# Differential attention blocks with the most keys: the second softmax is multiplied on ScalarE and added on GpSimd, and the build-time order is made anew

## The chip, the cores and the metric

The kernel runs on 1 core of one Trainium2 chip. The metric is device time in microseconds (us) of one execution; the value of a kernel is the median of its runs.

## The reference, cut to what matters

A decoder block over 2048 positions and 1024 features, all in float32: input projection, two kinds of attention side by side, output projection, and an MLP with squared ReLU. The change is in the attention alone, and there in the differential kind (4 heads), whose core is:

```python
s = jnp.einsum('bqhnd,bkhnd->bhnqk', q_i, k).astype(jnp.float32) * scale   # n = 0, 1: two score maps
s = s + bias[None, :, None]
s = jnp.where(mask, s, -jnp.inf)
p = jax.nn.softmax(s, axis=-1)
a = p[:, :, 0] - lam * p[:, :, 1]                                          # the "mix"
o = jnp.einsum('bhqk,bkhd->bqhd', a.astype(v.dtype), v)
o = rmsnorm(o, g_sub) * (1.0 - lam_init)
```

The other kind (forgetting attention, "FOX", 8 heads) has one softmax for each head and no mix.

## The kernel before, in words

**Stages.** Projection runs up to about 565 us, attention from there to about 1410 us, output projection to about 1640 us, and the MLP fills the rest. Nothing outside attention is touched.

**Blocks.** Attention is a list of 48 blocks (`attention_blocks`). There are 8 units u; even ones are FOX (a pair of heads, sides s = 0 and 1, a block for each), odd ones are differential (one head, a block for each J). A block is 512 queries, J = 0 to 3; block J needs 4 J + 4 key tiles of 128, so J = 3 is the longest. A FOX unit takes J in the order 0, 1, 2, 3, a differential unit 1, 3, 2, 0. There are four differential heads, so four differential blocks with J = 3: the "long differential blocks" that the change names. In a differential block each of the four query tiles a = 3, 2, 1, 0 (in this order) has `keys` = (4 J + a + 1) * 128 keys: 2048, 1920, 1792 and 1664 at J = 3.

**Steps of a block.** TensorE forms the scores of a tile in parts of at most 1024 columns ("score"); VectorE takes the negated row maximum from PSUM ("max", L1333); ScalarE writes exp into SBUF and sums it ("exp", L1294). The first softmax goes to `probs`, a ring of 141 * 128 columns; the second goes to `probs1`, which has two buffers. Where a tile has two parts, the low part's maximum is old: ScalarE makes a factor ("corr", L1274), and GpSimd multiplies the low 1024 columns of the first softmax by it ("fix", L1207). When both softmaxes of a differential tile are there, VectorE makes two factors out of sums and lambda ("chain", five instructions of one column, L1354 to L1362), and then the tile is mixed: probs += probs1 * factor ("mix"). For tiles a = 1, 2, 3 GpSimd mixes: multiply the high columns (L1216), multiply the low 1024 (L1219), add the high (L1222), add the low (L1226); L1229 and L1232 where a tile has one part. For tile a = 0 (`DVE_TILES`) VectorE mixes with one fused instruction for each part, high at L1371, low at L1376. Then, for each key tile, TensorE transposes the four query tiles into PSUM ("turn", L1458), ScalarE copies them to SBUF as the high half of a split product ("hi", L1303), VectorE subtracts for the low half ("lo", L1342), and TensorE multiplies by v ("pv", L1473 to L1478). Transposes, low halves and a few small steps share a ring of 3 PSUM banks; scores have 2 buffers; `p_hi` and `p_lo` have 4.

**What sets the order.** Each engine runs its own instruction stream in order, and a wait at the head of a stream holds all that stands behind it. The order in which the steps of different blocks are interleaved in these streams is made when the kernel is built, by a planner (`Walk`, L797 to L850): each step has an engine, a time for which it holds the engine, a time after which its result is there, predecessors, and an urgency. The planner walks through a model of time and lets each free engine take the able step with the lowest urgency. A step's urgency is its block's number, moved on with its place in the block, plus a constant of its kind (`RUSH`, L857); scores of long differential blocks are moved forward by `EARLY` blocks (L946). SP's stream (loads of q, k, v and stores) comes from the same walk. Steps of one kind keep their own order. The order alone comes out of the walk; correctness rests on semaphore waits that each engine makes for itself.

Of the kernel before, what the change touches and what calls it, by code (L numbers as in the profile page):

```python
# [8 lines left out]
ALU = mybir.AluOpType  # L9
# [727 lines left out]
DVE_TILES = (0,)  # L737

# [42 lines left out]
def probability_columns(blocks):  # L781

    places, former, owner, at = {}, {}, [None] * (PROB_COLUMNS // P), 0
    for b in blocks:
        for a in (3, 2, 1, 0):
            n = 4 * b.J + a + 1
            if (at + n) * P > PROB_COLUMNS:
                at = 0
            former[b.n, a] = max((o for o in owner[at:at + n] if o is not None), default=None)
            owner[at:at + n] = [b.n] * n  # L790
            places[b.n, a] = at * P
            at += n
    return places, former


class Walk:
# [18 lines left out]
    def order(self):  # L815
# [62 lines left out]
def attention_steps(blocks, scores, turns):  # L878
# [30 lines left out]
    def variance(b, urgency):  # L909

        before = diffs.index(b) - 1
        walk.step("var", b, "PE", 0.25, urgency, [("o_sq", b), ring[-TRING]], 0.45, line="ring")
        walk.step("o_var", b, "DVE", 0.2, urgency,
                  [("var", b), ("rows", b), ("o_pow", diffs[before]) if before >= 0 else None], line="ring")
        ring.append(("o_var", b))
        walk.step("o_pow", b, "POOL", 1.1, urgency,
                  [("o_var", b), ("spread", b.qb - 2) if b.qb >= 2 else None])

    def finish(q, urgency):

        pair = pairs[q]
        walk.step("spread", q, "PE", 0.5, urgency,
                  [("rows" if b.kind == FOX else "o_pow", b) for b in pair] + [ring[-TRING]],
                  0.7, line="ring")
        walk.step("o_scale", q, "DVE", 0.7, urgency, [("spread", q)] + [("o_add", b) for b in pair], line="ring")
# [16 lines left out]
    for b in blocks:  # L942
        ahead, mine, fox = by_block[b.n], turns_of[b.n], b.kind == FOX
        load("load_q", q_blocks[b.qb], b.n - 2, [("score", last_q[b.qb - 2])] if b.qb >= 2 else ())
        for k, sc in enumerate(ahead):
            at = b.n - 1 + SPREAD * k / len(ahead) - LEAD - (EARLY if not fox and b.J == 3 else 0)  # L946
            parts, two, keys = parts_of[b.n, sc.a, sc.s], sc.parts == 2, sc.lo + sc.width
            for p in pieces_of(sc):
                load_piece("load_k", b.u, p, b.n - 2)
            walk.step("score", sc, "PE", 0.00089 * sc.width + 0.03, at + RUSH["score"],  # L950
                      [("exp", scores[sc.g - 2]) if sc.g >= 2 else None, ("load_q", q_blocks[b.qb])]
                      + [("load_k", (b.u, p)) for p in pieces_of(sc)], 0.00089 * sc.width + 0.25)
            walk.step("max", sc, "DVE", 0.16 + 0.00104 * sc.width + (0.2 if sc.part else 0), at + RUSH["max"],
                      [("score", sc)])
            if sc.part:
                walk.step("corr", sc, "ACT", 0.29, at + RUSH["corr"], [("max", sc)])
# [9 lines left out]
            walk.step("exp", sc, "ACT", 0.49 + 0.00083 * sc.width, at + RUSH["exp"], after)  # L966
            if sc.part and (fox or sc.s == 0):
                walk.step("fix", (b.n, sc.a), "POOL", 2.0, at + RUSH["fix"], [("corr", sc), ("exp", parts[0])])
# [10 lines left out]
        for k, t in enumerate(mine):  # L979
# [3 lines left out]
            else:  # L983
# [4 lines left out]
            walk.step("turn", t, "PE", 0.0012 * width, at + RUSH["turn"], after, 0.0012 * width + 0.17, line="ring")  # L988
            walk.step("hi", t, "ACT", 0.2 + 0.00083 * width, at + RUSH["hi"],
                      [("turn", t), ("pv", turns[t.n - PRING]) if t.n >= PRING else None])  # L990
            walk.step("lo", t, "DVE", 0.16 + 0.00104 * width, at + RUSH["lo"], [("hi", t)], line="ring")
# [3 lines left out]
                      cost + 0.2)  # L995
# [6 lines left out]
        if fox:  # L1002
            walk.step("o_half", b, "ACT", 0.6, end, [("pv", mine[-1])])
        else:
            d = diffs.index(b)
            walk.step("o_sq", b, "ACT", 0.6, end, [("pv", mine[-1]), ("var", diffs[d - 1]) if d else None])
        walk.step("o_add", b, "DVE", 0.69, end, [("o_half" if fox else "o_sq", b),
                                                ("store", b.qb - ORING) if b.qb >= ORING else None])
# [17 lines left out]
def attend(nc, ctx, keep, qk, vals, q_rows, k_rows, mixT, w_out, x):  # L1026
# [22 lines left out]
    tile_no, chain_done, mix_done = {}, {}, {}  # L1049
    chains, mixes = 0, {True: 0, False: 0}  # L1050
    for sc in scores:
        if blocks[sc.b].kind == DIFF and sc.s == 1 and sc.part == sc.parts - 1:
            tile_no[sc.b, sc.a] = len(tile_no)
            chains += 5 if sc.parts == 2 else 2
            on_dve = sc.a in DVE_TILES
            mixes[on_dve] += (2 if sc.parts == 2 else 1) * (1 if on_dve else 2)
# [16 lines left out]
    with ExitStack() as own:  # L1073
# [34 lines left out]
        mixed = sems.sem("mixed")  # L1108
        mixed_dve = sems.sem("mixed_dve")
# [22 lines left out]
        def wait_mixed(eng, b, a):  # L1132
            eng.wait_ge(mixed_dve if a in DVE_TILES else mixed, mix_done[b, a])
# [58 lines left out]
        def gpsimd(pool):  # L1192
# [7 lines left out]
            for what, arg in steps:  # L1200
# [8 lines left out]
                elif what == "mix" and arg[1] not in DVE_TILES:  # L1209
# [58 lines left out]
        def scalar(act, then):  # L1268
            first_hi = next(arg for what, arg in steps if what == "hi")
            for what, arg in steps:  # L1270
# [5 lines left out]
                elif what == "exp":  # L1276
# [43 lines left out]
        def vector(dve, then, between):  # L1320
# [8 lines left out]
            for what, arg in steps:  # L1329
# [35 lines left out]
                elif what == "mix" and arg[1] in DVE_TILES:  # L1365
# [934 lines left out]
```

## Time and profile before

| | |
|---|---|
| Median of 3 runs | 3008.07 us |
| Lowest and highest of them | 3007.61 and 3008.24 us |
| The profiled execution's own time | 3007.83 us |
| Its span, first to last instruction | 3005.8 us |
| Granted TensorE clock, mean | 0.992 of full speed |
| TensorE busy | 2914.9 us (97%) |
| VectorE busy | 1660.9 us (55%) |
| ScalarE busy | 1022.1 us (34%) |
| GpSimd busy | 977.5 us (33%) |

How to read it: PE is TensorE's matmuls, PEld its weight loads, DVE VectorE, ACT ScalarE, POOL GpSimd. The shares are averages over stages that differ: the MLP alone fills nearly half of the span. So what bounds the attention stage has to be read from stretches of that stage.

### The profile page before, as it was taken

To read this page: it belongs to the slowest core of one execution; us is meant where nothing else is said; L and a number is where in the kernel's file an instruction comes from. 1 tells how busy PE (TensorE), PEld (TensorE's weight loads), DVE (VectorE), ACT (ScalarE), POOL (GpSimd) and SP (SyncE) were. 2 spreads that over 40 slices of the span, in tenths; PEclk is the share of its full clock that TensorE was granted. 3 is DMA by queue.
4 is the path that set the end of the run, shared out by engine and by line. 5 is a ranking of instruction groups with operands and counts; after the bars stand their busy time and mean duration, and the time that the engine had idled before them with its cause. 6 is when DMAs were issued, how large, how long until landed. Compare 5 with 4: busy or idle time off the path is not lost.

```text
span 3005.8 us, 39380 instructions
## 1 busy us (share of the span) xinstructions
PE 2914.9 (97%) x14130; PEld 2405.5 (80%) x14130; DVE 1660.9 (55%) x2505; ACT 1022.1 (34%) x1975; POOL 977.5 (33%) x720
## 2 busy tenths in 40 slices
PE   8999999998998999989999999999999999999998
PEld 6888888777877877777888888888887888888887
DVE  6111111389899898897556445444447544444455
ACT  5121111387786786875222111111112111111112
POOL 5120020157458365564114222212225221222222
PEclk9999999999999999999999999999999999999999
DMA  5342342833443344143762111111126111111103
GB/s 183 133 145 102 112 140 98 197 75 85 118 90 91 91 99 116 42 117 99 210 181 92 42 56 42 44 53 42 56 72 236 57 42 56 42 56 42 56 28 126
DMA packets 206425, 282.80 MB, mean 94 GB/s; under 512 B 12064, under 2 KB 136224, under 8 KB 206304
## 3 DMA queue, kind: packets, MB, share of 16 engines
q1 hardware_dynamic: 152160, 213.19, 25.0%
q10 hardware_dynamic: 53376, 67.25, 6.2%
q8 instruction: 71, 1.16, 0.2%
q0 software_dynamic: 768, 0.79, 0.1%
q14 instruction: 50, 0.41, 0.1%
HBM read 196.38 MB, written 84.80 MB: 94 GB/s over the span
## 4 chain that ended last, share of the span: by engine, by line
PE 67%; DVE 8%; issue 3%; ACT 2%; POOL 1%; ACTq 0%; DVEq 0%; POOLq 0%
PE ml_ps_u L2205 8%; PE ml_ps_u L2203 8%; PE ml_ps_u L2204 8%; PE ml_ps_y L2212 7%; PE ml_ps_y L2214 7%; PE ml_ps_y L2216 7%; PE at_ps_t L1458 4%; PE at_ps_s L1440 3%; PE at_ps_s L1434 3%; DVE at_nmax L1333 3%; PE at_ps_o L1473 2%; PE mo_acc L1774 2%; PE mo_acc L1776 2%; PE mo_acc L1775 2%; PE at_ps_o L1474 2%
## 5 line engine op out<-in xcount | busy, mean ns | idle before, releaser
L2163 DVE TENSOR_TENSOR ml_y<-ml_y,ml_ps_y 128x512 f32<-128x512 f32 x496 | 340.4, 686 | 219.0 <-PE ml_ps_y L2216 213.7
L2212 PE MATMUL ml_ps_y<-ml_dn_hi,ml_u_hi 128*128 128x512 f32 x992 | 389.5, 393 | 1.7 <-DVE ml_y L2163 1.7
L2214 PE MATMUL ml_ps_y<-ml_dn_lo,ml_u_hi 128*128 128x512 f32 x992 | 386.2, 389 | 0.0
L2216 PE MATMUL ml_ps_y<-ml_dn_hi,ml_u_lo 128*128 128x512 f32 x992 | 386.0, 389 | 0.0
L2203 PE MATMUL ml_ps_u<-h_rows_hi,ml_up_hi 128*128 128x512 f32 x992 | 385.9, 389 | 0.0
L2204 PE MATMUL ml_ps_u<-h_rows_lo,ml_up_hi 128*128 128x512 f32 x992 | 385.9, 389 | 0.0
L2205 PE MATMUL ml_ps_u<-h_rows_hi,ml_up_lo 128*128 128x512 f32 x992 | 385.9, 389 | 0.0
L1333 DVE TENSOR_REDUCE at_nmax<-at_ps_s 128x1 f32<-128x1024 f32 (+7 forms) x384 | 346.9, 906 | 48.8 <-PE at_ps_s L1440 44.4
L2120 DVE TENSOR_TENSOR ml_relu<-ml_relu 128x512 f32<-128x512 f32 x128 | 91.2, 712 | 467.7 <-ACT ml_relu L2079 467.7
L1980 POOL TENSOR_TENSOR ml_up_lo<-ml_up_raw,ml_up_hi 128x1024 fp32r<-128x1024 f32 x62 | 162.3, 2633 | 511.4 <-ACT ml_up_hi L2051 511.4
L1987 POOL TENSOR_TENSOR ml_dn_lo<-ml_dn_raw,ml_dn_hi 128x1024 fp32r<-128x1024 f32 x62 | 148.9, 2421 | 467.8 <-ACT ml_dn_hi L2069 467.8
L610 DVE SCALAR_TENSOR_TENSOR pj_out_sb<-pj_acc,pj_out_sb 128x512 fp32r<-128x512 f32 x96 | 66.3, 691 | 424.1 <-ACT pj_out_sb L546 424.1
L1342 DVE TENSOR_TENSOR at_p_lo<-at_ps_t,at_p_hi 128x512 fp32r<-128x512 f32 x480 | 280.2, 602 | 27.3 <-ACT at_p_hi L1303 25.6
L1458 PE MATMUL at_ps_t<-at_ident_r,at_probs 128*128 128x128 f32 x1632 | 251.1, 278 | 37.2 <-DVE at_p_lo L1342 32.2
L1303 ACT ACTIVATE at_p_hi<-at_ps_t 128x512 fp32r<-128x512 f32 x480 | 248.5, 531 | 92.2 <-PE at_ps_t L1458 59.6
L1294 ACT ACTIVATE at_probs<-at_ps_s,at_nmax 128x1024 f32<-128x1024 f32 (+7 forms) x256 | 237.4, 928 | 92.9 <-DVE at_nmax L1333 84.3
L2079 ACT ACTIVATE ml_relu<-ml_ps_u 128x512 f32<-128x512 f32 x128 | 76.7, 599 | 559.1 <-PE ml_ps_u L2205 545.0
L1458 PEld LDWEIGHTS at_ps_t<-at_ident_r,at_probs 128*128 128x128 f32 x1632 | 196.5, 143 | 82.6 <-issue 33.7
L2069 ACT ACTIVATE ml_dn_hi<-ml_dn_raw 128x1024 fp32r<-128x1024 f32 x62 | 62.4, 1051 | 562.7 <-PE ml_ps_y L2216 562.7
L1434 PE MATMUL at_ps_s<-at_k,at_q 128*128 128x512 f32 (+3 forms) x640 | 214.1, 400 | 17.1 <-ACT at_probs L1294 13.6
L1207 POOL TENSOR_TENSOR at_probs<-at_probs,at_corr 128x1024 f32<-128x1024 f32 x96 | 181.9, 1896 | 142.1 <-ACT at_corr L1274 142.1
L2212 PEld LDWEIGHTS ml_ps_y<-ml_dn_hi,ml_u_hi 128*128 128x128 f32 x992 | 186.2, 188 | 50.5 <-DVE ml_y L2163 12.8
(257 smaller groups left out, 5771.6 us busy)
## 6 DMA issues: line engine op xcount, KB each, us to landing
qk<-pj_out_sb ACTq DMA_DIRECT2D x64, 512.0 KB, 2.8
ml_dn_raw<-in_w_down_dram SPq DMA_DIRECT2D x32, 1024.0 KB, 4.9
ml_up_raw<-in_w_up_dram SPq DMA_DIRECT2D x31, 1024.0 KB, 5.4
at_q<-qk SPq DMA_DIRECT2D x96, 256.0 KB
at_k<-qk SPq DMA_DIRECT2D x96, 256.0 KB
vals<-pj_out_sb ACTq DMA_DIRECT2D x32, 512.0 KB, 2.9
at_v_sb<-vals SPq DMA_DIRECT2D x32, 512.0 KB, 3.9
pj_raw<-in_w_in_dram SPq DMA_DIRECT2D x24, 512.0 KB, 3.9
```

Source lines behind the costliest of these rows:

```text
L1303: act.activation(p_hi[:, t.n % PRING, t.off:512], ps_t[:, at % TRING, t.off:512], ACT.Copy)\
L1333: dve.tensor_reduce(nmax[:, par, sc.a, s, sc.part:sc.part + 1], ps_s[:, sc.g % 2, 0:sc.width], AX.X, ALU.max, negate=True).then_inc(maxed, 1)
L1342: dve.tensor_tensor(p_lo[:, t.n % PRING, t.off:512], ps_t[:, at % TRING, t.off:512], f32(p_hi[:, t.n % PRING, t.off:512]), ALU.subtract).t ...
L1434: pe.matmul(ps_s[:, sc.g % 2, at:at + width], q2[:, n, sc.s, q], k2[:, slot, sc.s, 0:width], start=True, stop=False)
L1458: last = pe.transpose(ps_t[:, at % TRING, a * P:(a + 1) * P], probs[:, key:key + P], ident)
L2163: dve.tensor_tensor(y[:, t, cols], y[:, t, cols], ps_y[:, b % 4, :], ALU.add)\
L2203: pe.matmul(ps_u[:, b % 4, :], up_h[:, k], h_hi[:, k, rows], start=(k == 0), stop=False)
L2204: pe.matmul(ps_u[:, b % 4, :], up_h[:, k], h_lo[:, k, rows], start=False, stop=False)
L2205: last = pe.matmul(ps_u[:, b % 4, :], up_l[:, k], h_hi[:, k, rows], start=False, stop=(k == KT - 1))
L2212: pe.matmul(ps_y[:, b % 4, :], u_hi[:, s, f, rows], hi[:, f, cols], start=(start and f == 0), stop=False)
L2214: pe.matmul(ps_y[:, b % 4, :], u_hi[:, s, f, rows], lo[:, f, cols], start=False, stop=False)
L2216: last = pe.matmul(ps_y[:, b % 4, :], u_lo[:, s, f, rows], hi[:, f, cols], start=False, stop=(stop and f == FT - 1))
```

## The change

It has two parts.

1. `scaled(b, a)` holds for all four tiles of differential blocks with J = 3. For these a new step "scale" on ScalarE waits for the chain and multiplies `probs1` in place by the factors, the high columns first and then the low 1024 (two Copy instructions with a scale for each row). The step "mix" is then two additions on GpSimd, for a = 0 as well: the high columns after the first scale, the low ones after the second scale and the fix. VectorE mixes no tile of these blocks. The blocks J = 0, 1, 2 keep GpSimd for a = 1, 2, 3 and VectorE for a = 0.
2. The planner's durations, the constants `RUSH`, and `SPREAD`, `LEAD`, `EARLY` are new, so that the order of all attention blocks is new.

The diff, cut:

```diff
+SCALED_TILES = (0, 1, 2, 3)
+def scaled(b, a):
+
+    return b.kind == DIFF and b.J == 3 and a in SCALED_TILES
+
+
+def on_vector(b, a):
+
+    return a in DVE_TILES and not scaled(b, a)
...
-RUSH = {"score": -0.98, "max": -0.24, "corr": 0.23, "exp": 0.27, "fix": -0.06, "chain": -0.22, "mix": 0.63,
-        "turn": 0.04, "hi": 0.14, "lo": -0.12, "pv": 0.25}
-SPREAD, LEAD, EARLY = 1.31, 0.45, 0.94
+RUSH = {"score": -1.113, "max": -0.06, "corr": 0.71, "exp": 0.362, "fix": 0.648, "chain": -1.388,
+        "mix": 0.875, "turn": 0.08, "hi": 0.131, "lo": -0.136, "pv": 0.259}
+SPREAD, LEAD, EARLY = 1.186, 0.433, 1.624
...
-            walk.step("exp", sc, "ACT", 0.49 + 0.00083 * sc.width, at + RUSH["exp"], after)
+            walk.step("exp", sc, "ACT", 0.24 + 0.00084 * sc.width, at + RUSH["exp"], after, 0.34 + 0.00084 * sc.width)
...
-                walk.step("chain", (b.n, sc.a), "DVE", 0.9 if two else 0.36, at + RUSH["chain"],
+                walk.step("chain", (b.n, sc.a), "DVE", 1.12 if two else 0.5, at + RUSH["chain"],
                           [("exp", sc), ("corr", sc) if two else None])
-                walk.step("mix", (b.n, sc.a), *(("DVE", 0.3 + 0.0016 * keys) if sc.a in DVE_TILES else
-                                                ("POOL", (0.8 if two else 0.4) + 0.0043 * keys)), at + RUSH["mix"],
-                          [("chain", (b.n, sc.a)), ("fix", (b.n, sc.a)) if two else None])
+                if scaled(b, sc.a):
+                    walk.step("scale", (b.n, sc.a), "ACT", 0.3 + 0.00084 * keys, at + RUSH["mix"], [("chain", (b.n, sc.a))])
+                    holder = "POOL", 0.15 + 0.0023 * keys
+                elif on_vector(b, sc.a):
+                    holder = "DVE", 1.5 if two else 0.1 + 0.0012 * keys
+                else:
+                    holder = "POOL", (0.8 if two else 0.4) + 0.0043 * keys
+                walk.step("mix", (b.n, sc.a), *holder, at + RUSH["mix"],
+                          [("scale" if scaled(b, sc.a) else "chain", (b.n, sc.a)), ("fix", (b.n, sc.a)) if two else None])
...
-            walk.step("turn", t, "PE", 0.0012 * width, at + RUSH["turn"], after, 0.0012 * width + 0.17, line="ring")
+            walk.step("turn", t, "PE", 0.00085 * width, at + RUSH["turn"], after, 0.00085 * width + 0.16, line="ring")
...
+                elif what == "mix" and scaled(blocks[arg[0]], arg[1]):
+                    n, at, low = arg[0], places[arg], 1024
+                    keys = (4 * blocks[n].J + arg[1] + 1) * P
+                    one = probs1[:, tile_no[arg] % 2, :]
+                    pool.wait_ge(multiplied, scale_done[arg] - 1)
+                    pool.tensor_tensor(probs[:, at + low:at + keys], probs[:, at + low:at + keys], one[:, low:keys],
+                                       ALU.add).then_inc(mixed, 1)
+                    pool.wait_ge(multiplied, scale_done[arg])
+                    pool.wait_ge(fixed, fix_no[arg])
+                    pool.tensor_tensor(probs[:, at:at + low], probs[:, at:at + low], one[:, 0:low],
+                                       ALU.add).then_inc(mixed, 1)
...
+                elif what == "scale":
+                    (n, a), par, low = arg, arg[0] % SETS, 1024
+                    keys = (4 * blocks[n].J + a + 1) * P
+                    one = probs1[:, tile_no[arg] % 2, :]
+                    act.wait_ge(chained, chain_done[arg])
+                    act.activation(one[:, low:keys], one[:, low:keys], ACT.Copy,
+                                   scale=factor[:, par, a, 0:1]).then_inc(multiplied, 1)
+                    act.activation(one[:, 0:low], one[:, 0:low], ACT.Copy,
+                                   scale=factor[:, par, a, 1:2]).then_inc(multiplied, 1)
```

The other durations (score, max, corr, fix, hi, lo, pv, var, spread, o_add and so on) change in the same manner; most steps now have a holding time and a longer result time. `mix_done`, `scale_done` and the waits on them follow from `scaled` and `on_vector`.

## Rows read from the trace of the kernel before

**Rows 1.** The page: span, and busy time, share and instructions of each engine.

```profile
span 3005.8 us, 39380 instructions
PE 2914.9 (97%) x14130; PEld 2405.5 (80%) x14130; DVE 1660.9 (55%) x2505; ACT 1022.1 (34%) x1975; POOL 977.5 (33%) x720
```

**Rows 2.** Busy time by stretch: stretch, busy us (instructions) by engine, granted clock, DMA.

```profile
590.00:1400.00 810.00, 750.05 (x4453) 624.68 (x4453) 725.59 (x1316) 616.78 (x1394) 483.33 (x363) 0.98 0.38 93
...
650.00:700.00 50.00, 47.56 (x277) 38.84 (x277) 46.92 (x77) 41.81 (x85) 30.03 (x23) 1.00 0.53 118
700.00:750.00 50.00, 41.90 (x233) 34.33 (x231) 45.55 (x86) 33.20 (x77) 40.91 (x25) 0.93 0.26 71
750.00:800.00 50.00, 48.30 (x315) 41.94 (x314) 42.68 (x91) 35.68 (x90) 23.03 (x24) 1.00 0.62 150
900.00:950.00 50.00, 41.28 (x229) 33.80 (x230) 46.77 (x87) 34.23 (x77) 40.95 (x23) 0.93 0.26 69
1100.00:1150.00 50.00, 41.27 (x222) 33.56 (x221) 46.51 (x83) 33.96 (x75) 35.85 (x21) 0.90 0.30 80
1300.00:1350.00 50.00, 40.60 (x214) 32.12 (x213) 46.96 (x81) 34.96 (x75) 35.46 (x20) 0.94 0.29 80
```

**Rows 3.** TensorE in order of time: start, duration, [idle before <-releaser].

```profile
729.25 1.09 PE L1458 MATMUL at_ps_t<-at_ident_r,at_probs 128*128 128x128 f32 x4 [5.63 <-DVE at_p_lo L1342]
...
1346.38 1.08 PE L1458 MATMUL at_ps_t<-at_ident_r,at_probs 128*128 128x128 f32 x4 [5.63 <-DVE at_p_lo L1342]
```

**Rows 4.** VectorE and then GpSimd in order of time, around 721 to 727 us.

```profile
721.65 4.66 DVE L1371 SCALAR_TENSOR_TENSOR at_probs<-at_probs,at_factor 128x640 f32<-128x640 f32 x1
726.23 1.27 DVE L1376 SCALAR_TENSOR_TENSOR at_probs<-at_probs,at_factor 128x1024 f32<-128x1024 f32 x1
...
721.33 2.40 POOL L1226 TENSOR_TENSOR at_probs<-at_probs 128x1024 f32<-128x1024 f32 x1
723.67 1.91 POOL L1207 TENSOR_TENSOR at_probs<-at_probs,at_corr 128x1024 f32<-128x1024 f32 x1
725.52 0.85 POOL L1260 TENSOR_TENSOR at_squares<-at_total 128x4 f32<-128x4 f32 x1
```

**Rows 5.** The same two engines around 760 us, at the block J = 2.

```profile
760.84 0.34 DVE L1371 SCALAR_TENSOR_TENSOR at_probs<-at_probs,at_factor 128x128 f32<-128x128 f32 x1
761.10 1.28 DVE L1376 SCALAR_TENSOR_TENSOR at_probs<-at_probs,at_factor 128x1024 f32<-128x1024 f32 x1
...
758.06 2.41 POOL L1226 TENSOR_TENSOR at_probs<-at_probs 128x1024 f32<-128x1024 f32 x1
760.42 0.21 POOL L1260 TENSOR_TENSOR at_squares<-at_total 128x4 f32<-128x4 f32 x1
```

**Rows 6.** Busy time by stretch, as in Rows 2, in steps of 5 us.

```profile
725.00:730.00 5.00, 0.75 (x5) 0.79 (x5) 4.97 (x7) 1.21 (x2) 1.37 (x2) 0.67 0.03 5
730.00:735.00 5.00, 5.00 (x25) 4.51 (x24) 3.00 (x8) 2.66 (x6) 0.00 (x0) 0.65 0.01 3
```

**Rows 7.** Groups by line and shape: count | busy us, mean ns | idle before.

```profile
L1371 DVE SCALAR_TENSOR_TENSOR at_probs<-at_probs,at_factor 128x640 f32<-128x640 f32 x4 | 18.6, 4652 | 0.0
L1376 DVE SCALAR_TENSOR_TENSOR at_probs<-at_probs,at_factor 128x1024 f32<-128x1024 f32 x8 | 10.2, 1274 | 0.0
L1219 POOL TENSOR_TENSOR at_probs<-at_probs,at_factor 128x1024 f32<-128x1024 f32 x24 | 45.5, 1897 | 0.0
L1226 POOL TENSOR_TENSOR at_probs<-at_probs 128x1024 f32<-128x1024 f32 x24 | 57.4, 2390 | 0.0
L1222 POOL TENSOR_TENSOR at_probs<-at_probs 128x1024 f32<-128x1024 f32 x4 | 9.6, 2404 | 0.0
L1222 POOL TENSOR_TENSOR at_probs<-at_probs 128x768 f32<-128x768 f32 x4 | 7.4, 1840 | 0.0
```

**Rows 8.** A ScalarE copy from SBUF to SBUF of the MLP, from the page's groups.

```profile
L2069 ACT ACTIVATE ml_dn_hi<-ml_dn_raw 128x1024 fp32r<-128x1024 f32 x62 | 62.4, 1051 | 562.7 <-PE ml_ps_y L2216 562.7
```

**Rows 9.** Busy time by stretch: around the first long differential block, and the busiest for ScalarE.

```profile
690.00:750.00 60.00, 50.52 (x282) 41.22 (x281) 55.17 (x105) 41.10 (x94) 46.50 (x27) 0.94 0.26 70
...
1250.00:1300.00 50.00, 49.36 (x296) 41.19 (x296) 46.20 (x73) 43.47 (x90) 30.39 (x26) 1.00 0.39 98
```

More of the change, by code:

```diff
@@ L911, in variance @@
         before = diffs.index(b) - 1
-        walk.step("var", b, "PE", 0.25, urgency, [("o_sq", b), ring[-TRING]], 0.45, line="ring")
-        walk.step("o_var", b, "DVE", 0.2, urgency,
-                  [("var", b), ("rows", b), ("o_pow", diffs[before]) if before >= 0 else None], line="ring")
+        walk.step("var", b, "PE", 0.43, urgency, [("o_sq", b), ring[-TRING]], 0.58, line="ring")
+        walk.step("o_var", b, "DVE", 0.08, urgency,
+                  [("var", b), ("rows", b), ("o_pow", diffs[before]) if before >= 0 else None], 0.16, line="ring")
         ring.append(("o_var", b))
@@ L921, in finish @@
         pair = pairs[q]
-        walk.step("spread", q, "PE", 0.5, urgency,
+        walk.step("spread", q, "PE", 0.44, urgency,
                   [("rows" if b.kind == FOX else "o_pow", b) for b in pair] + [ring[-TRING]],
-                  0.7, line="ring")
-        walk.step("o_scale", q, "DVE", 0.7, urgency, [("spread", q)] + [("o_add", b) for b in pair], line="ring")
+                  0.6, line="ring")
+        walk.step("o_scale", q, "DVE", 0.61, urgency, [("spread", q)] + [("o_add", b) for b in pair], 0.69, line="ring")
         ring.append(("o_scale", q))
@@ L994, in attention_steps @@
                       [("lo", t), ("load_v", (b.u, t.j // 4)), ("o_add", blocks[b.n - 1]) if k == 0 and b.n else None],
-                      cost + 0.2)
+                      cost + 0.16)
             advance(at)
@@ L1048, in attend @@
                                               if sc.part == 1 and (blocks[sc.b].kind == FOX or sc.s == 0))}
-    tile_no, chain_done, mix_done = {}, {}, {}
-    chains, mixes = 0, {True: 0, False: 0}
+    tile_no, chain_done, mix_done, scale_done = {}, {}, {}, {}
+    chains, mixes, scales = 0, {True: 0, False: 0}, 0
     for sc in scores:
@@ L1054, in attend @@
             chains += 5 if sc.parts == 2 else 2
-            on_dve = sc.a in DVE_TILES
-            mixes[on_dve] += (2 if sc.parts == 2 else 1) * (1 if on_dve else 2)
+            on_dve, on_act = on_vector(blocks[sc.b], sc.a), scaled(blocks[sc.b], sc.a)
+            mixes[on_dve] += (2 if sc.parts == 2 else 1) * (1 if on_dve or on_act else 2)
+            scales += 2 if on_act else 0
+            scale_done[sc.b, sc.a] = scales
             chain_done[sc.b, sc.a] = chains
@@ L1108, in attend @@
         mixed = sems.sem("mixed")
+        multiplied = sems.sem("multiplied")
         mixed_dve = sems.sem("mixed_dve")
@@ L1132, in wait_mixed @@
         def wait_mixed(eng, b, a):
-            eng.wait_ge(mixed_dve if a in DVE_TILES else mixed, mix_done[b, a])
+            eng.wait_ge(mixed_dve if on_vector(blocks[b], a) else mixed, mix_done[b, a])
         def side(sc):
@@ L1208, in gpsimd @@
                         .then_inc(fixed, 1)
-                elif what == "mix" and arg[1] not in DVE_TILES:
+                elif what == "mix" and scaled(blocks[arg[0]], arg[1]):
[9 more added lines that the diff above has]
+                                       ALU.add).then_inc(mixed, 1)
+                elif what == "mix" and not on_vector(blocks[arg[0]], arg[1]):
                     (n, a), par, at = arg, arg[0] % SETS, places[arg]
@@ L1364, in vector @@
                     assert links[0] == chain_done[arg]
-                elif what == "mix" and arg[1] in DVE_TILES:
+                elif what == "mix" and on_vector(blocks[arg[0]], arg[1]):
                     (n, a), par, at = arg, arg[0] % SETS, places[arg]
```

26 lines of the change are left out of this document (13 added, 13 removed).

## The prediction

> **What bounds the kernel now.** I read the page first [rows 1]: TensorE is busy 97% of the span, which says that little is to be had and nothing of where. Then busy time by stretch [rows 2]. The attention stage, 590 to 1400 us, is another picture: TensorE 750 of 810 us, VectorE 726, ScalarE 617, GpSimd 483. So 60 us of TensorE idleness lie here, with VectorE at 90% as the second engine. The idleness is not even. In 750 to 800 us TensorE has 48.3 of 50 us and the full clock; in the four stretches that hold the long differential block of a head (700, 900, 1100, 1300) it has 40.6 to 41.9, and the granted clock is 0.90 to 0.94. VectorE is at 45.6 to 47.0 there.
>
> TensorE's own timeline [rows 3] gives the reason: once in each head it idles 5.6 us at a stretch (5.63, 5.65, 5.58 and 5.63 us; first and last are shown), released each time by a "lo" of VectorE. VectorE's timeline at that place [rows 4] shows what stands in front of these "lo": the mix of tile a = 0. Its high part, 640 columns, takes 4.66 us; the low part of 1024 columns takes 1.27. A smaller operation cannot need more work than a larger one, so it waited. GpSimd runs back to back beside it (an add from 721.33, a fix from 723.67 to 725.58), and VectorE's instruction ends at 726.31, 0.7 us behind the fix. At the J = 2 block the same two lines take 0.34 and 1.28 us [rows 5], and there GpSimd's long add has ended at 760.47, before they start at 760.84. So the reading is that a VectorE instruction with both tensor inputs in SBUF waits while GpSimd works on SBUF, here through two GpSimd instructions, and with it wait all "max" and "lo" behind it, and so both TensorE and ScalarE (ScalarE is busy 1.21 of 5 us in 725 to 730 [rows 6]). The Trainium skill ("SBUF — State Buffer", section "SBUF: two separate sides") says that VectorE with two SBUF inputs and GpSimd take a shared port pair as an exclusive lock for a whole instruction. By that rule, the trace agrees, with 4.66 us for 640 columns.
>
> **Part 1a: the stall goes.** Removed from VectorE: four L1371 at 4.65 us and four L1376 at 1.27 us, that is 18.6 + 5.1 = 23.7 us [rows 7], 5.9 us for each head. TensorE's stall of 5.6 us is on the path that sets the end, since every engine but GpSimd is starved in it: 22.5 us for four.
>
> **Part 1b: the clock after it.** TensorE's granted clock falls during the idle time. The means of 0.67 and 0.65 in 725 to 735 us [rows 6] mean the 1.2 GHz level for 3.3 and 3.5 us of the 5. TensorE is back at 729.25 [rows 3], so about 0.75 + 3.5 = 4.2 us of its work go at half speed, a loss of 2.1 us. Over the four stretches of 50 us the deficit is 0.07 + 0.07 + 0.10 + 0.06 = 0.30 x 50 = 15 us of clock [rows 2]; with some 5 to 6 us of it inside the idle times (1.3 in the first), 9 us were lost in work. If nothing takes the stall's place, 22.5 + 9 = 31.5 us come back, 7.9 for each head. This is the upper bound of part 1.
>
> **Part 1c: GpSimd.** It loses the multiplies of a = 1 to 3 (three of 1.90 us and three of high columns by about 1.90 x 768/1024 = 1.42 to 1.90: 10.7 us for each head) and gains the adds of a = 0: 2.39 low, and for 640 columns 1.84 - (2.40 - 1.84)/2 = 1.56 high, together 3.95 us [rows 7]. Net 6.7 us less in a stretch where it has 46.5 of 60 us [rows 9]. I cost it at nothing; the last tile's additions of 3.95 us are behind the last scale, where 5.9 us of VectorE mixing were before, and other blocks' transposes cover them. Without this cover the price is 3.95 us for each head.
>
> **Part 1d: ScalarE.** It gains 8 instructions for each head. A copy from SBUF to SBUF of 1024 columns takes 1.05 us [rows 8]; the high parts have 640 to 1024 columns, 832 in the mean, about 0.88 us. So 4 x (1.05 + 0.88) = 7.7 us for each head, 31 us in all. This is not free. Take 690 to 750 us [rows 9] as the stretch in which it lands. Before: VectorE 55.2, ScalarE 41.1, TensorE 50.5. After: VectorE 55.2 - 5.9 = 49.3, ScalarE 41.1 + 7.7 = 48.8, TensorE 50.5 - 2.1 = 48.4. All three want about 49 us. VectorE reaches 94% in 650 to 700 us [rows 2]; at 94% it needs 52.4 us, a gain of 7.6. ScalarE's busiest stretch shows 43.5 of 50, or 87% [rows 9]; if it can't do better, it needs 56.1 us, a gain of 3.9. So part 1 is worth 3.9 to 7.9 us for each head. The new scores of the long block are to begin 0.7 blocks sooner (EARLY 0.94 to 1.62), which spreads ScalarE's new work over a longer time; over the whole of attention ScalarE then has 617 + 31 = 648 us of some 783, or 83%. I take 6.5 us, somewhat above the middle: 26 us.
>
> The Trainium skill ("ScalarE: Activation LUTs", section "What ACT_TABLE_LOAD costs") has a rule against the change: an operand that is one value for each partition, as this scale is, adds about 93 ns to an instruction. No row before has a copy with such a scale from SBUF; by the page the sum would be 32 x 0.093 = 3 us more of ScalarE, and at 87% some 3 us less of gain.
>
> **Added waits.** The scale waits for VectorE's chain at the head of ScalarE's stream, and behind it stand exps and "hi". The chain is five small instructions, about 1.2 us, and has the new urgency of -1.39, so VectorE takes it at once in the plan; where the plan errs by a microsecond, ScalarE stands idle for it. 16 scales: from 0 to 16 us together, and it is inside the range of 3.9 to 7.9 for each head. GpSimd's wait for the scale holds the next fix behind it. The next exp of the second softmax waits for the mix two tiles before, as it did; the mix is no later, for the same reason as in part 1c.
>
> **Part 2: the new order.** No row shows it. Outside the four stalls 60 - 22.5 = 37.5 us of TensorE idleness are left in attention. A plan whose durations are nearer to the trace could take a part, a worse guess could add as much. Bounds: a third of it each way, 12 us. SP's loads move with the scores; DMA is at a share of 0.26 in these stretches, so I cost them at nothing; if a load of keys came late, it would show as a TensorE wait at the scores. I take 0 for the value.
>
> **Sum.** Profiled execution 3007.8 us (0.2 below the median of the runs) - 26 = 2981.8; against the median 2982.
>
> **The rivals.**
> 1. The forecast: stalls gone, half-clock stretches gone, ScalarE gives back a part. 2974 to 2990 us. Chance 0.47.
> 2. The same, and the new order takes up a part of the other idleness: 3008 - 30 - 12 = 2966 us. For it: the old plan gave a mix on VectorE no price for GpSimd's work, and an exp 0.49 us beside its columns; errors of that kind are everywhere in it. Against it: in 750 to 800 us TensorE is at 97% already [rows 2]. Chance 0.20.
> 3. ScalarE, or GpSimd's wait for it, is the new bound in the long blocks: 3.9 us or less for each head, and the order costs a little: 2992 to 3000 us. For it: 48.8 us of work in some 52. Chance 0.17.
> 4. Slower. The stall moves to the J = 2 blocks. Their tile a = 0 is still mixed on VectorE, and before it missed GpSimd's last long add by 0.37 us only [rows 5]. In a new order with chains and mixes at other urgencies, VectorE can come to it while GpSimd is in its row of multiplies and adds of tile a = 1 or of a fix behind it. Its price would be the one of rows 4, 3.9 us of waiting and a 5.6 us stall with the clock, 7.9 for each head, which eats 31 us against the 26 won: 3013 us. It decides the sign if it occurs in all four heads with the full length, or in three if ScalarE holds back too. As the plan is the same in each head, all four or none is likely. Chance 0.08.
> 5. Within 0.2% (6 us, about what a measurement of this kernel can tell from no change): a smaller collision at J = 2, or at J = 1, and a saturated ScalarE together, 3006 us. Chance 0.08. That the change doesn't do what it says is no more than a case of this: the scaled tiles follow from J and a alone.
>
> The Trainium skill ("Perfetto Trace Analysis", section "Optimizing Scalar/DVE Operations") warns that moving work between GpSimd and VectorE might not help, because of the shared port. That is rival 4's mechanism, and by it the J = 2 blocks' tile would be hit; the one trace here has it unhurt at 1.28 us.
>
> **How the numbers follow.** 2982 is the likeliest case's. The range reaches from rival 2 to rival 3: 2963 to 3001. Faster by over 0.2%: 0.47 + 0.20 + 0.17 = 0.84; within 0.08; slower 0.08.
>
> **What would show it.** Right: no L1371 of 128x640; L1376 of 1024 columns four times only; no TensorE wait over 3 us between 600 and 1400 us; the granted clock 1.00 in all stretches of 50 us there; ScalarE copies of about 1.05 and 0.9 us at the new lines; ScalarE near or over 45 of 50 us at the long blocks. TensorE's idle time in attention down from 60 to about 40 us. Wrong: a 128x128 or 128x1024 mix of VectorE with several microseconds at J = 2; ScalarE idle in front of a scale, released by VectorE's factor; TensorE's transposes released by GpSimd's add.

## The result, and the profile after

| | before | after |
|---|---|---|
| Median of 4 runs each, in turn on one chip | 3008.15 us | 2986.64 us |
| Lowest and highest | 3007.61, 3008.65 | 2985.57, 2987.83 |
| Profiled execution: time, span | 3007.83, 3005.8 | 2987.83, 2986.1 |

The change saves 21.5 us. The ratio is 0.9929, with a 95% interval of 0.9911 to 0.9946. All of it lies in attention: from the last matmul with v to the end, both traces have 1606 us (1605.7 and 1606.2); attention's last such matmul ends at 1379.9 us instead of 1400.1.

Busy time by stretch of the kernel after, to be held beside [rows 2]:

```profile
590.00:1380.00 790.00, 745.94 (x4459) 619.07 (x4460) 705.79 (x1309) 644.38 (x1430) 457.46 (x347) 1.00 0.38 96
...
650.00:700.00 50.00, 48.50 (x284) 39.58 (x282) 47.23 (x77) 43.58 (x88) 29.94 (x23) 1.00 0.54 124
700.00:750.00 50.00, 45.49 (x258) 36.34 (x259) 45.00 (x97) 42.62 (x94) 39.44 (x24) 1.00 0.27 75
750.00:800.00 50.00, 48.10 (x318) 42.29 (x318) 42.62 (x86) 35.59 (x89) 21.53 (x24) 1.00 0.65 156
...
900.00:950.00 50.00, 45.69 (x251) 36.57 (x250) 43.51 (x94) 41.42 (x92) 38.10 (x23) 0.97 0.28 75
```

TensorE has 45.5 to 45.7 us in the four stretches of long blocks, where it had 40.6 to 41.9; its idle time in attention is 790 - 746 = 44 us, where it was 60. ScalarE, the fourth of the busy times, went from 33.2 to 42.6 us in 700 to 750.

TensorE in order of time, its idle times of 1.1 us and more around the long block of the first two heads [rows 3]:

```profile
714.05 0.74 PE L1474 MATMUL at_ps_s<-at_k,at_q 128*128 128x512 f32 x2 [1.17 <-ACT at_probs L1325]
758.69 1.20 PE L1498 MATMUL at_ps_t<-at_ident_r,at_probs 128*128 128x128 f32 x9 [1.13 <-DVE at_probs L1416]
...
913.31 0.73 PE L1474 MATMUL at_ps_s<-at_k,at_q 128*128 128x512 f32 x2 [1.17 <-ACT at_probs L1325]
959.58 1.20 PE L1498 MATMUL at_ps_t<-at_ident_r,at_probs 128*128 128x128 f32 x9 [1.14 <-DVE at_probs L1416]
```

The 5.6 us are gone. A head now takes (1359.15 - 758.69)/3 = 200.2 us (1359.15 is the same wait in the fourth head); before it took (1346.38 - 729.25)/3 = 205.7 us [rows 3]. Four times 5.5 is 22 us: the whole gain, which is 20.2 us by the end of attention in the two traces and 21.5 by the medians.

The groups that answer to [rows 7] and [rows 8]: the scales (L1332, L1334), GpSimd's additions of the long blocks (L1234, L1238), and VectorE's mix of the J = 1 blocks:

```profile
L1334 ACT ACTIVATE at_probs<-at_probs,at_factor 128x1024 f32<-128x1024 f32 x16 | 18.2, 1141 | 0.0
...
L1238 POOL TENSOR_TENSOR at_probs<-at_probs 128x1024 f32<-128x1024 f32 x16 | 40.6, 2539 | 0.0
...
L1234 POOL TENSOR_TENSOR at_probs<-at_probs 128x640 f32<-128x640 f32 x4 | 6.3, 1568 | 4.6 <-ACT at_probs L1332 4.6
...
L1416 DVE SCALAR_TENSOR_TENSOR at_probs<-at_probs,at_factor 128x640 f32<-128x640 f32 x4 | 6.1, 1517 | 0.0
```

A scale of 1024 columns takes 1.14 us, 0.09 more than the copy of [rows 8]. The Trainium skill's page "ScalarE: Activation LUTs" (section "What ACT_TABLE_LOAD costs") gives 93 ns for an operand that is one value for each partition; this row agrees, with 1141 ns against 1051.

### The profile page after: what moved, and what is told of

Same layout as the page of the kernel before. It is cut to its first block, busy times and chain, and to the rows that moved or that the text cites. A ratio compares the mean times of both kernels' runs of the same rounds, so it can differ in the third digit from the quotient of the medians.

```text
span 2986.1 us, 39392 instructions
## 1 busy us (share of the span) xinstructions
PE 2911.2 (97%) x14130; PEld 2399.2 (80%) x14130; DVE 1640.3 (55%) x2497; ACT 1048.5 (35%) x2007; POOL 951.8 (32%) x704
## 4 chain that ended last, share of the span: by engine, by line
PE 68%; DVE 5%; ACT 4%; issue 3%; POOL 1%; ACTq 0%; DVEq 0%; POOLq 0%
PE ml_ps_u L2245 8%; PE ml_ps_u L2244 8%; PE ml_ps_u L2243 8%; PE ml_ps_y L2252 7%; PE ml_ps_y L2254 7%; PE ml_ps_y L2256 7%; PE at_ps_t L1498 5%; PE at_ps_s L1474 3%; PE at_ps_s L1480 3%; PE mo_acc L1814 2%; PE mo_acc L1816 2%; PE mo_acc L1815 2%; PE at_ps_o L1513 2%; PE at_ps_o L1514 2%; ACT at_probs L1325 1%
```

## Experiments

All are compared with the kernel before, run beside them on the same chip (3007.2 to 3008.0 us).

### The two halves of the change, each alone

`order_only`: new planner, no tile scaled.

```diff
-SCALED_TILES = (0, 1, 2, 3)
+SCALED_TILES = ()
```

> The changed kernel with no tile scaled: new durations and constants, the long blocks mixed as before (GpSimd for a = 1 to 3, VectorE for a = 0). Theory (the gain is the stall of VectorE's mix under GpSimd's work): L1371's form of 128x640 is still there and still takes some microseconds, TensorE still idles 4 to 6 us once a head, and the time is 3000 to 3008 us, ratio 0.998 to 1.000. Rival (the gain is the new order): no stall over 3 us, and at or below 2995 us, ratio 0.996 or less.

`mix_only`: all tiles of the long blocks scaled; the durations of all other steps, RUSH, SPREAD, LEAD and EARLY as before. The scale and its additions are in the plan with the change's durations.

> The scaled mix of the long blocks with the durations and constants of the planner before. Theory: the stall is gone without the new order, and most of the 21.5 us too: 2988 to 2994 us, ratio 0.9935 to 0.9955. Rival (the new order is needed, because the old one puts ScalarE's scale where an exp is urgent): over 3000 us, ratio over 0.9975.

`gpsimd_alone`: planner as before, no scale, GpSimd multiplies and adds all four tiles. The line that does it, against mix_only (whose tiles are no longer scaled either):

```diff
-    return a in DVE_TILES and not scaled(b, a)
+    return a in DVE_TILES and b.J < 3
```

> The planner before (its durations and constants); the tile a = 0 of long blocks is mixed by GpSimd alone as the others are, ScalarE gets nothing. Theory (ScalarE is not needed for the stall, only VectorE's instruction has to go): VectorE's stall is gone, but GpSimd gains 7.2 us a head in a stretch where it is the busiest but one, so that tile's transposes and the next fix come later: 2990 to 3000 us, ratio 0.994 to 0.9975. Rival (GpSimd's time is what sets the long blocks): 3008 us or more.

| kernel | median us | ratio, 95% interval |
|---|---|---|
| order_only | 3032.83 | 1.0081 [1.0067, 1.0094] |
| mix_only | 3008.71 | 1.0001 [0.9992, 1.0010] |
| gpsimd_alone | 3011.45 | 1.0012 [1.0003, 1.0021] |

None came out as the theory had it. Each half alone gains nothing, and the order alone costs 25 us; only together they save 21.5. gpsimd_alone came out as its rival had it: GpSimd is busy 49.4 of 50 us in 700 to 750, so it has no room there for the mix of a fourth tile with its multiplications. What TensorE waited for in 590 to 1400 us, in total, times and longest, in mix_only:

```profile
PE at_ps_t L1498 <- DVE at_p_lo L1382: 31.2, 34, 2.5
PE at_ps_s L1474 <- ACT at_probs L1325: 10.1, 21, 0.6
```

in the kernel before:

```profile
PE at_ps_t L1458 <- DVE at_p_lo L1342: 32.2, 22, 5.7
```

and in order_only:

```profile
PE at_ps_s L1474 <- ACT at_probs L1325: 30.4, 22, 2.6
PE at_ps_t L1498 <- DVE at_probs L1416: 13.3, 7, 2.8
```

No wait of 5.6 us in either. In mix_only the wait for "lo" has nearly the total that it had before the change, 31 us against 32 (of which the four stalls were 22.5), in pieces of 2.5 us and less. In order_only VectorE's 640-column mix takes 0.93 us in all four long blocks, so the new order by itself had moved it out of GpSimd's way but for the last 0.2 us of a fix, and paid for that with scores that wait for exps and with transposes that wait 13.3 us for VectorE's other mixes (L1416). One of these, the 640 columns of the J = 1 blocks, takes 2.18 us in the mean there, where it took 1.31 before. The stall was gone in three kernels, and the time was not.

### Is the reading of the stall right, and what is the stall worth?

`short_fix`: the kernel before; one fix of GpSimd, the one beside VectorE's long instruction, works on 16 columns in each of the four heads.

```diff
+                    if (blocks[n].kind, blocks[n].J, a) == (DIFF, 2, 3):
+                        low = probs[:, places[n, a]:places[n, a] + 16]
```

> The kernel before, in which GpSimd's fix of the J = 2 block's tile a = 3, which ran beside VectorE's 4.66 us instruction, works on 16 columns instead of 1024 (the low probabilities of that tile are left uncorrected beyond them). Theory (VectorE waits for GpSimd's SBUF work): the 128x640 mix of VectorE falls from 4.65 us by about 1.7 us to some 2.9 us, TensorE's idle time before the transposes from 5.6 to about 4 us, and the kernel is 6 to 8 us faster (fixes four times shorter). Rival (the 640-column instruction is slow for a cause of its own): it stays at 4.65 us.

A single run: 3001.26 us, 6.5 less than the kernel before. VectorE in order of time, and GpSimd:

```profile
723.40 2.81 DVE L1373 SCALAR_TENSOR_TENSOR at_probs<-at_probs,at_factor 128x640 f32<-128x640 f32 x1
...
723.08 2.38 POOL L1228 TENSOR_TENSOR at_probs<-at_probs 128x1024 f32<-128x1024 f32 x1
725.42 0.87 POOL L1209 TENSOR_TENSOR at_probs<-at_probs,at_corr 128x16 f32<-128x16 f32 x1
```

The mix fell from 4.65 us to 2.84 in the mean of four, and the wait of TensorE from 5.62 to 3.81. As expected, VectorE waits for GpSimd, and 4 x 1.8 = 7.3 us of stall were worth 6.5 us.

`short_mix` and `one_column`: the kernel before, in the same order; VectorE's two mixes in each long block become two scalings of 16 columns, and of one.

```diff
+                    if blocks[n].J == 3:
+                        for lo in (1024, 0):
+                            if lo == 0:
+                                dve.wait_ge(fixed, fix_no[arg])
+                            dve.tensor_scalar(probs[:, at + lo:at + lo + 16], probs[:, at + lo:at + lo + 16],
+                                              factor[:, par, a, 0:1], None, ALU.mult).then_inc(mixed_dve, 1)
+                        continue
```

> The kernel before, same order, in which VectorE's two mix instructions of long blocks are two scalings of 16 columns with one tensor input (the second softmax is left out of tile a = 0 of those blocks). Nothing is added anywhere, so this is the bound of part 1 of the change. Theory: the prediction's 31.5 us less, 2974 to 2982 us, ratio 0.989 to 0.9915. Rival (the score loop or the order holds most of it back): over 2992 us, ratio over 0.995.

> short_mix once more, with one column in place of 16: VectorE's small chain instructions of one column take 0.27 us beside GpSimd, while the two of 16 columns took 4.16 us together and so still waited for it. The order is the one of the kernel before, nothing is added, and the second softmax is left out of tile a = 0 of the long blocks. This is the bound of part 1 that short_mix did not give. Theory (a stall in an unchanged order is worth its full length and the clock's): TensorE's wait of 5.6 us falls under 1 us, the granted clock is 1.00 at the long blocks, 2974 to 2984 us, ratio 0.989 to 0.992; then what mix_only and same_order lost, they lost to the scale and the later additions. Rival (another wait of a similar length stands behind the first): 2990 us or more, ratio 0.994 or more.

short_mix took 2999.73 us (0.9973 [0.9962, 0.9984]) and missed its purpose: the instructions with 16 columns waited too. one_column took 2982.24 us (0.9915 [0.9901, 0.9928]). The same place on VectorE, first in short_mix:

```profile
722.32 4.16 DVE L1374 TENSOR_SCALAR at_probs<-at_probs,at_factor 128x16 f32<-128x16 f32 x2
```

and in one_column, whose busy time by stretch is below it (the last stretch is its whole attention stage):

```profile
721.10 0.32 DVE L1374 TENSOR_SCALAR at_probs<-at_probs,at_factor 128x1 f32<-128x1 f32 x2
```

```profile
700.00:750.00 50.00, 46.56 (x274) 38.24 (x273) 46.43 (x101) 38.71 (x90) 46.45 (x28) 1.00 0.31 86
...
590.00:1372.70 782.70, 741.20 (x4453) 616.98 (x4452) 703.40 (x1315) 616.67 (x1393) 480.77 (x363) 1.00 0.39 97
```

In one_column the clock stays at 1.00 in the long blocks and the span is 2978.3 us, 27.5 less than before; by medians 25.7 less, as its theory had it. Against [rows 2], TensorE is idle 41.5 us in attention where it was 60, 18.5 less, and the same 4453 matmuls keep it busy for 741.2 us where it was 750.1, 8.9 less at the higher clock. So in an unchanged order the stall with its half-clock time was worth 26 to 27.5 us (with it went VectorE's own work in the two instructions, and the wait of the transposes for their result). It was real. What ate it in mix_only is the next question.

### What takes the gain back

`same_order`: the order of the kernel before, step for step; the scale goes into ScalarE's stream where the mix stood.

```diff
-    steps = attention_steps(blocks, scores, turns)
+    steps = []
+    for what, arg in attention_steps(blocks, scores, turns):
+        if what == "mix" and scaled(blocks[arg[0]], arg[1]):
+            steps.append(("scale", arg))
+        steps.append((what, arg))
```

> The scaled mix in the order of the kernel before, step for step: the planner plans with VectorE's mix as it did, and each scale is put into ScalarE's stream just ahead of its mix. Theory (the stall is worth what the profile says as long as the order around it stays; mix_only lost it because taking VectorE's mix out of the plan moved other steps into waits): 2980 to 2992 us, ratio 0.991 to 0.995. Rival (the stall is hidden time: without it the score loop of the long blocks, 35 us a head in every version so far, sets the pace): 3000 us or more, ratio over 0.9975.

3007.73 us (0.9999 [0.9990, 1.0008]). Here the order of all other steps is the one of one_column, so the two differ by the real mix: about 25.5 us by medians, 28.3 by the spans. (The mix of all four tiles is scaled in same_order; one_column leaves the mix of a = 0 out and has the other three on GpSimd.) The rival's number came, but not its cause: one_column had shown that no score loop holds the time back. TensorE's waits in 590 to 1400 us in same_order,

```profile
PE at_ps_s L1472 <- ACT at_probs L1323: 27.8, 34, 1.6
PE at_ps_t L1496 <- DVE at_p_lo L1380: 9.1, 14, 1.9
...
PE at_ps_t L1496 <- POOL at_probs L1236: 4.8, 4, 1.2
```

and in one_column:

```profile
PE at_ps_s L1441 <- ACT at_probs L1294: 13.2, 27, 0.9
PE at_ps_t L1465 <- DVE at_p_lo L1342: 12.3, 22, 1.9
```

Scores wait 14.6 us longer for exps, and the transposes of the long block wait 4 x 1.2 us for GpSimd's last addition, a wait that one_column has not; the waits for "lo" are 3.2 us shorter. That is 16 us net. The rest is clock, as the whole attention stage of same_order shows:

```profile
590.00:1400.70 810.70, 752.56 (x4456) 624.07 (x4456) 706.08 (x1309) 645.31 (x1430) 454.32 (x347) 0.99 0.38 94
```

TensorE is idle 58.1 us, 16.6 more than in one_column, and busy 11.4 us longer for as many matmuls; the granted clock is 0.96 or 0.97 in the four stretches of long blocks, where one_column has 1.00. How an exp comes late is seen on ScalarE in same_order, in order of time:

```profile
707.41 1.03 ACT L1330 ACTIVATE at_probs<-at_probs,at_factor 128x896 f32<-128x896 f32 x1
708.34 1.13 ACT L1332 ACTIVATE at_probs<-at_probs,at_factor 128x1024 f32<-128x1024 f32 x1
709.38 0.88 ACT L1323 ACTIVATE at_probs<-at_ps_s,at_top 128x768 f32<-128x768 f32 x1
...
710.41 0.61 PE L1472 MATMUL at_ps_s<-at_k,at_q 128*128 128x512 f32 x2 [1.46 <-ACT at_probs L1323]
```

The exp stands 2 us behind two scales, it frees one of only two score buffers, and TensorE waits 1.46 us for it (the last line). That the scales' place in the stream is the cause is read from such rows; no run shortened the scales in this order.

`short_scale_old` and `short_scale`: each scale of mix_only, and of the changed kernel, cut to 16 columns; 0.30 us each instead of 1.14. Order as in the one and the other.

```diff
-                    act.activation(one[:, 0:low], one[:, 0:low], ACT.Copy,
+                    act.activation(one[:, 0:16], one[:, 0:16], ACT.Copy,
```

> The scaled mix under the old planner (mix_only, which took 3008.7 us), with each scale cut to 16 columns, the order being the same; the second softmax is then scaled in those columns only. Theory A (in the old order the stall's time is given back because 'hi' and exp wait behind 2 us of scale on ScalarE): about 30 us less of ScalarE comes out of the chain in the long blocks, and the time falls to 2978 to 2990 us, ratio 0.990 to 0.994. Rival B (given back because GpSimd's additions or the order of scores hold TensorE): over 3000 us, ratio over 0.9975.

> The changed kernel, with each scale cut to 16 columns, same order; the second softmax is then scaled in those columns only. Theory A (ScalarE is what bounds the long blocks after the change, some 10 us short of the 31.5 us bound): 2972 to 2980 us, ratio 0.988 to 0.991. Rival B (VectorE or TensorE bound them): within 3 us of 2986.6 us, ratio 0.992 to 0.994.

3005.79 us (0.9995 [0.9985, 1.0004]) and 2987.84 us (0.9933 [0.9917, 0.9948]). Both missed the time of theory A. In mix_only the reading is plain: ScalarE has 18 us less to do in 590 to 1400 us, TensorE's waits stay as they were (31.4 us for "lo", 10.4 for exps), and the time falls by 2 to 3 us. So the length of the scales is not what mix_only lost; what is left is the order, or GpSimd's additions, and no run parts these two.

In the changed kernel, where ScalarE's busy time went from 653 to 629 us, the equal time hides two effects. TensorE's waits in the changed kernel, and behind them in short_scale:

```profile
PE at_ps_s L1474 <- ACT at_probs L1325: 12.5, 26, 1.2
PE at_ps_t L1498 <- DVE at_p_lo L1382: 8.0, 21, 0.5
...
PE at_ps_t L1498 <- DVE at_p_lo L1382: 15.3, 18, 2.6
PE at_ps_s L1474 <- ACT at_probs L1325: 5.8, 9, 1.2
```

The waits for exps fell by 6.7 us, and those for "lo" rose by 7.3. The rise is a new collision of VectorE with GpSimd. With short scales GpSimd's additions begin 2.2 us sooner (694.31 instead of 696.51 us), and VectorE's mix of 640 columns at J = 1 starts as the second of them starts. In short_scale, VectorE and then TensorE:

```profile
696.69 3.01 DVE L1416 SCALAR_TENSOR_TENSOR at_probs<-at_probs,at_factor 128x640 f32<-128x640 f32 x1
...
700.36 1.11 PE L1498 MATMUL at_ps_t<-at_ident_r,at_probs 128*128 128x128 f32 x4 [2.61 <-DVE at_p_lo L1382]
```

The mix takes 3.01 us where it took 1.52 in the changed kernel, and TensorE waits 2.6 us at that place instead of 0.5, in all four heads: 8.4 us. In three of the four heads the granted clock falls behind this wait, to 0.50, 0.66 and 0.68 in the next 5 us; in the second head it stays at 1.00. So short_scale does not show that the scales cost nothing; by these rows their length was worth some 8 us, which the collision took back. That is an estimate from the waits; no run has short scales without the collision.

### The planner

With the scaled mix in all of them: `new_durations` has the new durations and the old constants, `new_constants` the reverse, `rounded` is the changed kernel with

```diff
-RUSH = {"score": -1.113, "max": -0.06, "corr": 0.71, "exp": 0.362, "fix": 0.648, "chain": -1.388,
-        "mix": 0.875, "turn": 0.08, "hi": 0.131, "lo": -0.136, "pv": 0.259}
-SPREAD, LEAD, EARLY = 1.186, 0.433, 1.624
+RUSH = {"score": -1.1, "max": -0.1, "corr": 0.7, "exp": 0.4, "fix": 0.6, "chain": -1.4,
+        "mix": 0.9, "turn": 0.1, "hi": 0.1, "lo": -0.1, "pv": 0.3}
+SPREAD, LEAD, EARLY = 1.2, 0.4, 1.6
```

> The changed kernel with the old RUSH, SPREAD, LEAD, EARLY and the new durations in the planner. Theory A (the durations read from the trace are what makes room for the scale): 2986 to 2995 us, ratio 0.993 to 0.996. Rival B (the constants carry it, since they say what goes first on ScalarE and VectorE): 3002 us or more, ratio over 0.998.

> The changed kernel with the old durations in the planner and the new RUSH, SPREAD, LEAD, EARLY. Theory A (durations): 3002 us or more, ratio over 0.998. Rival B (constants): 2986 to 2995 us, ratio 0.993 to 0.996. If both this and new_durations are slow, the constants were fitted to the durations and only the pair works.

> The changed kernel with RUSH, SPREAD, LEAD and EARLY rounded to one decimal (each moved by 0.05 at most). Theory (the new constants were fitted, and the order is a rough function of them): 5 to 25 us slower than the changed kernel, 2992 to 3012 us, ratio 0.9945 to 1.001. Rival (what counts is the broad sense of the constants, chains first and long blocks early): within 3 us of 2986.6 us, ratio 0.992 to 0.994.

| scaled mix, and | old constants | new constants | new, rounded |
|---|---|---|---|
| old durations | 3008.71 (mix_only) | 3043.61 | |
| new durations | 3003.01 | 2986.64 (the change) | 3048.15 |

Ratios: new_durations 0.9984 [0.9975, 0.9993], new_constants 1.0118 [1.0102, 1.0133], rounded 1.0132 [1.0117, 1.0148]. The new durations under the old constants give 5 us. So neither part alone carries the gain, as the expectation of new_constants had named it. The constants belong to these durations and this mix: with other durations they cost 35 us over the old constants, without the scaled mix (order_only) 25 over the kernel before, and moved by 0.05 at most they cost 61 us, which is far outside both ranges expected for rounded. So no broad sense of them carries the gain.

In rounded the prediction's rival 4 is to be seen (in new_constants too, where the 1024 columns take 2.34 us). VectorE's mixes at J = 1 and J = 2:

```profile
L1416 DVE SCALAR_TENSOR_TENSOR at_probs<-at_probs,at_factor 128x640 f32<-128x640 f32 x4 | 10.0, 2497 | 0.0
L1416 DVE SCALAR_TENSOR_TENSOR at_probs<-at_probs,at_factor 128x1024 f32<-128x1024 f32 x4 | 9.4, 2351 | 0.0
L1411 DVE SCALAR_TENSOR_TENSOR at_probs<-at_probs,at_factor 128x128 f32<-128x128 f32 x4 | 3.5, 885 | 0.0
```

The 1024 columns at J = 2 take 2.35 us in the mean instead of 1.27, and the 128 columns 0.89 instead of 0.34. That is 4 x 1.6 = 6.5 us of VectorE's time, and 4 x 1.0 more at J = 1 (2.50 instead of 1.52 in the changed kernel): 10.5 us in all, a sixth of the 61 us; what followed from it for TensorE and its clock was not priced. TensorE's waits in attention are longer than in the changed kernel by 18 us for exps (30.6 against 12.5), 9 for "lo" (17.2 against 8.0) and 6 for VectorE's mixes (10.2 against 4.5), each at most 2.5 us long.

## Why the prediction was right, and where it was not

2982 us was forecast with 2963 to 3001, and 2986.6 was measured. The sum was 26 us and came to 21.5. The stall and its cause were as forecast. That the number came close is luck in part: the loss that the replacement brings depends on the order, from all of the gain to a few microseconds, and the forecast had no row for either.

- **The stall (part 1a), right.** Its cause is shown by short_fix: with GpSimd's fix cut to 16 columns VectorE's instruction took 1.81 us less, about the 1.9 us of a full fix. All waits over 3 us are gone from attention in the changed kernel.
- **Stall and clock (parts 1a and 1b), 31.5 us as upper bound: 4 to 6 us too much.** one_column has 25.7 us by medians, 27.5 by the spans of the profiled executions. The part put too high is 1a: 22.5 us of idle time were to go, and 18.5 went, since other waits grew in their place, those for "lo" by 2.6 us and those for exps by 1.6. The clock was right: 9 us forecast, 8.9 measured.
- **GpSimd (part 1c), "I cost it at nothing", wrong in the old order.** The last additions were to be covered by other blocks' transposes; in same_order TensorE waits for them once a head, 1.2 us, of the 3.95 named as the price without cover. In the changed kernel TensorE has no such wait.
- **ScalarE (part 1d), right in size as far as the rows tell, incomplete in kind.** The prediction took its 7.7 us a head as a share of a stretch that all engines fill, and so a loss of 1.4 us a head, 5.5 in all. In the new order the waits for exps are 6.7 us longer with full scales than with short ones, and the collision that short_scale runs into hides what that was worth; nothing there speaks against 5.5. What the prediction lacked is that the price depends on the place in the stream. In the old order the real mix takes back all that the stall's end gives, 25.5 us (same_order against one_column), by the rows through exps that stand behind scales while TensorE has two score buffers, through the additions above, and through the clock. This was argued from rows and not tried by a run.
- **The new order (part 2), 0 with 12 us each way, the step that failed.** With the same mix, the new plan is 21 us faster than the old order (same_order to the change, by ratios 0.9999 and 0.9929), and other plans of the same planner are up to 61 us slower. Counted this way, 26 were won, 26 given back, and 21 won by the plan; the forecast had 31.5, 5.5 and 0. The parts don't add up in one way only: with the order first, it costs 25 us (order_only), and the mix then wins 46.
- **The rivals.** The time falls in the forecast's case, 2974 to 2990 us; its mechanism, a small loss on ScalarE, fits the rows of the changed kernel but leaves out the part of the order. Rival 2 had the part of the truth that the order is worth many microseconds. Rival 4 did not occur: the J = 2 blocks' mixes stayed at 0.34 and 1.28 us. At J = 1 the 640 columns take 1.52 us, but they met GpSimd before the change as well, with 1.31 us, against some 0.87 without a meeting (an estimate between the 0.34 us of 128 columns and the 1.27 of 1024 in [rows 5] and [rows 7]).
- **The signs named.** Idle time of TensorE: "about 40 us", measured 44. ScalarE at "near or over 45 of 50 us": 42.6, too high. The clock "1.00 in all stretches": 0.97 in 900 to 950 and 1300 to 1350 us; it falls at 930 to 940 us (0.81 and 0.85) and at 1330 to 1340 us (0.75 and 0.91), around a wait of TensorE of 1.1 us; in the two other heads the same wait, at 732 and 1132 us, stands in stretches with 1.00, so what decides is open. ScalarE never waits for the chain at a scale; the cost named for that, 0 to 16 us, is 0.

What in the new plan makes the room for the scale was not isolated. The short scale ran into a collision, no single step's duration was tried alone, and of the constants only all together were.

## What to carry to other kernels

A stall that the profile shows can be priced by shortening its cause in an unchanged order (here by one column in place of 640 and 1024), before anything is put in its place; that run tells what is to be had, and the run with the replacement in the same order tells what it costs. In such a run look at the waits by kind and not at the time alone: in short_scale an equal time hid a wait that had gone and another that had come, because a shortened instruction lets other engines start sooner and meet elsewhere. Where each engine's order is fixed at build time, an engine's busy share alone does not give the price of a new instruction: the same scales went with no gain at all in one order and with 21.5 us in another. Ask who stands behind it, and how few buffers wait for that. Such an order is fitted to the instructions it was made for, so a change of an instruction is to be judged with a plan made for it, and not by the old one.

## What the runs showed of the hardware

- VectorE instructions wait for GpSimd's SBUF work with one tensor input as well: two scalings of 16 columns, float32 from SBUF to SBUF, took 4.16 us together beside a GpSimd row that ended at 726.25 us, while those of one column took 0.32 us beside the same GpSimd instructions (2.07 and 0.20 us for one in the mean of eight). The prediction had the wait for two tensor inputs only. What makes the difference between 16 columns and one was not tried.
- VectorE's waiting instruction did not get its turn between two GpSimd instructions that followed each other directly: 4.65 us through an addition and a fix [rows 4]. That is not always so, as the next rows show. In short_fix VectorE's instruction ended at 726.21 us, 0.75 us behind the addition (725.46), and the fix of 16 columns behind it took 0.87 us, where one of 4 columns (L1260) takes 0.20 in one_column: by these rows VectorE went ahead of the short fix.
- In short_scale VectorE's mix (696.69 to 699.70 us, shown above) met an addition (696.65 to 699.02) with a fix right behind it, and ended 0.68 us behind the addition; the fix took 2.49 us instead of 1.90. So here VectorE had its turn between the two. What decides it was not found.
- The wait goes both ways. In the changed kernel GpSimd's addition beside VectorE's mix at J = 1 takes longer than the 2.39 us of [rows 7]; VectorE first, then GpSimd, in order of time:

```profile
698.05 1.52 DVE L1416 SCALAR_TENSOR_TENSOR at_probs<-at_probs,at_factor 128x640 f32<-128x640 f32 x1
...
696.51 2.37 POOL L1234 TENSOR_TENSOR at_probs<-at_probs 128x1024 f32<-128x1024 f32 x1 [4.99 <-ACT at_probs L1332]
698.84 2.96 POOL L1238 TENSOR_TENSOR at_probs<-at_probs 128x1024 f32<-128x1024 f32 x1
```

By these rows VectorE came in between two additions: the first ended at 698.88 us, VectorE's instruction at 699.57, and the second addition took 0.57 us more than its mean of 2.39.
